# Layer 1's expert loop: the up product in three rounded products instead of one full product, with its halves added by GpSimd

## What is computed

```python
def _peer(h, w_q, sub_keys, expert_u, expert_v):
    ...
        act = jax.nn.gelu(jnp.einsum('td,thkd->thk', tb, expert_u[idx]).astype(jnp.float32),
                          approximate=False)
        w = (gate * act).astype(tb.dtype)
        return jnp.einsum('thk,thkd->td', w, expert_v[idx])
```

## Time and profile before

| what | us |
| --- | --- |
| three runs | 2755.24, 2757.75, 2752.68 (median 2755.24) |
| the profiled execution, own time | 2755.3 |
| its span in the trace | 2753.3 |
| layer 1's expert loop, first to last matmul | 2158.9 to 2732.4 |
| PE busy in the span | 2614.4 (95%) |
| DVE busy | 2260.7 (82%) |
| ACT busy | 1200.7 (44%) |
| POOL busy | 476.4 (17%) |

### The profile page before, as it was taken

The page is one execution under the profiler, slowest core; times in us unless marked ns, Lnnn a source line. Parts: engine busy times, 40 slices in busy tenths (PEclk is TensorE's granted clock), DMA queues, the critical chain, the costliest instruction groups (busy, mean ns, idle before and its releaser), DMA issues.

```text
span 2753.3 us, 48491 instructions
## 1 busy us (share of the span) xinstructions
PE 2614.4 (95%) x16733; PEld 2275.8 (83%) x16733; DVE 2260.7 (82%) x4474; ACT 1200.7 (44%) x2189; POOL 476.4 (17%) x428
## 2 busy tenths in 40 slices
PE   7999999877799999999999998999989999999998
PEld 5878887556788888888888886888979888888887
DVE  6478664999899999999999997797689777777665
ACT  5344442226844444444444445334426533333332
POOL 0000000004533333333333330000004211110010
PEclk8999999888999999999999999999999999999999
DMA  6522322554499999999999993333443699999895
GB/s 268 226 83 98 119 77 107 233 204 143 153 341 371 387 389 386 387 392 382 380 362 370 368 363 139 108 131 104 169 150 134 249 337 340 337 338 329 321 323 200
DMA packets 172367, 708.89 MB, mean 257 GB/s; under 512 B 17088, under 2 KB 50528, under 8 KB 124896
## 3 DMA queue, kind: packets, MB, share of 16 engines
q1 hardware_dynamic: 134480, 431.60, 42.4%
q0 software_dynamic: 37776, 275.83, 27.0%
HBM read 690.61 MB, written 16.65 MB: 257 GB/s over the span
## 4 chain that ended last, share of the span: by engine, by line
PE 81%; DVE 12%; DMA 3%; ACT 2%; issue 2%; SPq 0%; DVEq 0%; ACTq 0%
PE ps L969 81%; DMA ring<-in_w_mod 1%; DVE topi L2675 1%; DVE topi L2683 1%; DVE sc L2677 1%; DMA ring<-in_w_front 1%; DVE top L2680 1%; DVE top L2672 1%; DMA gate_scratch<-spill 1%; DVE elo L2264 0%; DVE rs L2224 0%; DVE loP L2333 0%; DVE gst L2488 0%; PE ps L1121 0%; DVE besti L2683 0%
## 5 line engine op out<-in xcount | busy, mean ns | idle before, releaser
L894 POOL DMA_INDIRECT gbuf<-in_expert_rows,gidx x192 | 277.0, 1443 | 1097.0 <-DVE yg L2846 1080.3
L969 PE MATMUL ps<-h2a,ehi 128*128 128x320 f32 x2048 | 453.0, 309 | 0.0
L2176 ACT ACTIVATE ehi<-ring 128x1024 fp32r<-128x1024 f32 x256 | 271.2, 1059 | 400.0 <-PE ps L969 350.9
L2858 DVE TENSOR_TENSOR elo<-ring,ehi 128x1024 fp32r<-128x1024 f32 x256 | 313.6, 1225 | 136.5 <-ACT ehi L2176 132.2
L969 PE MATMUL ps<-ehi,wA 128*128 128x512 f32 x1280 | 377.2, 392 | 3.5 <-DVE wA L2893 3.5
L969 PE MATMUL ps<-h2b,ring 128*128 128x192 f32 x2048 | 359.7, 326 | 1.0 <-ACT act_ahead L2049 1.0
L969 PEld LDWEIGHTS ps<-h2a,ehi 128*128 128x128 f32 x2048 | 347.7, 188 | 10.3
L969 PEld LDWEIGHTS ps<-h2b,ring 128*128 128x128 f32 x2048 | 338.2, 190 | 10.5 <-issue 1.3
L969 PE MATMUL ps<-h2a,elo 128*128 128x320 f32 x1024 | 316.4, 309 | 0.0
L969 PEld LDWEIGHTS ps<-ehi,wA 128*128 128x128 f32 x1280 | 236.2, 189 | 54.0 <-DVE wA L2893 3.7
L2836 DVE SCALAR_TENSOR_TENSOR gbuf<-gbuf,h2n 128x1024 f32<-128x1024 f32 x192 | 234.4, 1221 | 31.2 <-DMA gbuf<-in_expert_rows,gidx 25.1
(11 more groups left out here) (445 smaller groups left out, 4797.0 us busy)
## 6 DMA issues: line engine op xcount, KB each, us to landing
ring<-in_experts SPq DMA_DIRECT2D x512, 512.0 KB, 6.9
ring<-in_w_mod SPq DMA_DIRECT2D x48, 1024.0 KB, 6.5
ring<-in_w_side SPq DMA_DIRECT2D x24, 1024.0 KB, 5.2
ring<-in_w_front SPq DMA_DIRECT2D x12, 1024.0 KB, 7.5
ring<-in_w_merge SPq DMA_DIRECT2D x16, 768.0 KB, 4.3
ring<-in_w_q SPq DMA_DIRECT2D x12, 1024.0 KB, 7.7
gate_scratch<-spill SPq DMA_DIRECT2D x40, 256.0 KB, 2.0
gateA<-gate_scratch SPq DMA_DIRECT2D x16, 640.0 KB, 8.6
```

The lines of the kernel that those rows point to most:

```text
L894: pool.indirect_dma_start(gbuf[:, k % 2, :], None, a[f"expert_rows{l}"], bass.IndirectOffsetOnAxis(gidx[:, at:at + 1], 0)).then_inc(gather ...
L969: return pe.matmul(out, w, x, start=start, stop=stop, **k)
L2176: act.activation(ehi[:, 2 + k % 2, :], ring[:, (u + k) % RING, DM:2 * DM], ACT.Copy).then_inc(vhi_ready, 1)
L2858: v.tensor_tensor(elo[:, r, DM:2 * DM], ring[:, r, DM:2 * DM], ehi[:, 2 + b, :].bitcast(F32), ALU.subtract).then_inc(vlo_ready, 1)
```

## The change

1. **Up in layer 1** is computed from parts. `h2c` holds the rounded tokens and their remainder side by side. For each of the eight chunks PE does one fp32r matmul of 384 columns (rounded weights against both halves of the tokens) and one of 192 columns (remainder weights against the rounded half). The result stands in 384 columns of PSUM, in two halves that have yet to be added.
2. **ACT** gets `u_high` in layer 1 (the rounded copy of the up weights), and `carry(k + 1)` at the end of step k, which copies the 384 columns from PSUM to `upB`. **POOL** adds the two halves into `actB` and signals `summed`. ACT's Gelu then waits for `summed`.
3. **DVE** gets `u_low` in layer 1. The rounded copy of the gated activations (CAST, 128x192) goes from DVE to ACT, as in layer 0, with the handshake `act_gated` and `whi_ready`. The remainder stays in two operations.
4. **POOL**'s queue holds the additions and gathers in one order: for odd k, gather k // 2 + 2 stands behind the addition of block k.
5. **Constant products** (`keep_on`): bf16 matmuls of 512 columns on the identity, whose result nobody reads, at three kinds of place: 26 behind the mean of layer 1's `norm1`, 12 behind the mean of `norm2` (layer 0's latent pass and layer 1), 8 at the end of layer 0's experts.
6. Before the loop DVE writes `h2c` (two more operations in `norm2`, one copy at the start of `experts`). Buffers move. The semaphores of the two constant loads become one.

```diff
@@ POOL, experts
-                    for k in range(2, gathers(l)):
+                    for k in range(NK if l else 0):
+                        if not is_ahead(l, k):
+                            pool.wait_ge(carried, ups_before(l, k) - NK + 1)
+                            count(pool, w_ready, NK * l + k - 1)
+                            pool.tensor_tensor(actB[:, k % 2, :], upB[:, 0, :], upB[:, 1, :], ALU.add).then_inc(summed, 1)
+                        if k % 2 and k // 2 + 2 < gathers(l):
+                            pool.wait_ge(acc_done, gathers_before(l) + k // 2 + 1)
+                            gather(l, k // 2 + 2)
+                    for k in range(2, 0 if l else gathers(l)):
@@ PE
+            def keep_on(n, bank):
+                one = ident.bitcast(BF16)
+                for _k in range(n):
+                    mm(ps[:, bank, :].rearrange("p (a n) -> p a n", a=2), one[:, 0:P], one.unsqueeze(1).to_broadcast([P, 2, 256]), True, True)
@@ PE, up
+                        pe.wait_ge(ulo_ready, i * per + (ups_before(l, k) + 1))
+                        hi, lo_ = ehi[:, k % 2, :], elo[:, v % RING, 0:DM]
                         if l:
-                            pe.wait_ge(u_in[v % RING], i * 16 + 16 * u_loads(l, k))
                             for c in range(KD):
-                                last = mm(o, ring[:, v % RING, c * P:(c + 1) * P], h2[:, c, :], c == 0, c == KD - 1)
+                                s_ = slice(c * P, (c + 1) * P)
+                                both_ = ps[:, 6 + k % 2, 0:2 * D].rearrange("p (a t) -> p a t", a=2)
+                                mm(both_, hi[:, s_], h2[:, :, c, :], c == 0, False)
+                                last = mm(o, lo_[:, s_], h2[:, 0, c, :], False, c == KD - 1)
@@ ACT, experts
+                    def carry(k, i, per):
+                        act.wait_ge(a_ready, i * per + (ups_before(l, k) + 1))
+                        act.activation(upB[:, :, :], ps[:, 6 + k % 2, 0:384].rearrange("p (a t) -> p a t", a=2), ACT.Copy).then_inc(carried, 1)
@@ ACT, step
+                            if l:
+                                act.wait_ge(summed, i * (RING - is_ahead(l, first)) + (ups_before(l, k) - ub + 2))
+                                act.activation(actT[:, k % 2, :], actT[:, k % 2, :], ACT.Gelu).then_inc(act_ready, 1)
...
-                        if ahead and not l:
-                            u_high(k + 2, i)
-                        if not l:
-                            act.wait_ge(act_gated, i * RING + (k + 1))
-                            act.activation(wh[:, k % 2, :], actT[:, k % 2, :], ACT.Copy).then_inc(whi_ready, 1)
+                        if ahead and not is_ahead(l, k + 2):
+                            u_high(k + 2, i, RING - is_ahead(l, first))
+                        act.wait_ge(act_gated, i * RING + (ub + k + 1))
+                        act.activation(wh[:, k % 2, :], actT[:, k % 2, :], ACT.Copy).then_inc(whi_ready, 1)
...
+                        if l and k + 1 < NK and not is_ahead(l, k + 1):
+                            carry(k + 1, i, RING - is_ahead(l, first))
@@ DVE, norm2
-                        v.tensor_copy(h2[:, :, :], h2T[:, :, 0:w]).then_inc(h2_ready, 1)
+                        v.tensor_copy(h2b[:, :, :], h2T[:, :, 0:w]).then_inc(h2_ready, 1)
+                        link(v.tensor_copy(h2c[:, 1, :, :], h2T[:, :, 0:w]))
+                        v.tensor_tensor(h2c[:, 1, :, :], h2T[:, :, 0:w], h2c[:, 1, :, :].bitcast(F32), ALU.subtract)
@@ DVE, step
-                        if l:
-                            link(v.tensor_tensor(w_, from_, g, ALU.mult))
-                            link(v.tensor_copy(wh[:, b, :], actT[:, b, :]))
-                        else:
-                            v.tensor_tensor(w_, w_, g, ALU.mult).then_inc(act_gated, 1)
-                            if ahead:
-                                u_low(k + 2, i)
-                            dve.wait_ge(whi_ready, i * RING + (k + 1))
+                        v.tensor_tensor(w_, from_ if l else w_, g, ALU.mult).then_inc(act_gated, 1)
+                        if ahead and not is_ahead(l, k + 2):
+                            u_low(k + 2, i, RING - is_ahead(l, first))
+                        dve.wait_ge(whi_ready, i * RING + (ub + k + 1))
@@ DVE, experts
                         dve.wait_ge(ahead_act, AHEAD)
+                        v.tensor_copy(h2c[:, 0, :, :], h2b[:, :, :]).then_inc(h2_ready, 1)
+                        u_low(1, 0)
```

More of the change, by code:

```diff
@@ L436, in build_program @@
         first = ExitStack()
-        h2b = sb("h2b", [P, KD, 192], on=first)
+        lend = ExitStack()
+        h2b = sb("h2b", [P, KD, 192], on=lend)
+        lend.close()
+        h2c = sb("h2c", [P, 2, KD, 192], F32R, on=first)
         idxB = sb("idxB", [P, 3, 192], on=first)
-        actB = sb("actB", [P, 2, 192], on=first)
-        wB = sb("wB", [P, 2, 384], F32R, on=first)
-        whB, wlB = wB[:, :, 0:192], wB[:, :, 192:384]
         act_ahead = sb("act_ahead", [P, IN_ROUTE, 192], on=first)
         first.close()
-        sb("first_space", [P, KD * 2 * DENSE + DM + NK // SLOTS], on=peer)
+        sb("first_space", [P, (2 * KD + 3 + IN_ROUTE) * 192], on=peer)
         h2n = sb("h2n", [P, DM], on=peer)
@@ L455, in build_program @@
         act_more = sb("act_more", [P, AHEAD - IN_ROUTE, 192], on=over)
+        actB = sb("actB", [P, 2, 192], on=over)
         over.close()
@@ L461, in build_program @@
         zeros = sb("zeros", [P, P], on=lend)
+        wB = sb("wB", [P, 2, 384], F32R, on=lend)
+        whB, wlB = wB[:, :, 0:192], wB[:, :, 192:384]
+        upB = sb("upB", [P, 2, 192], on=lend)
         lend.close()
@@ L568, in build_program @@
             sem("lo_ready"), sem("fwh_ready"), sem("fwl_ready"), sem("swh_ready"), sem("swl_ready"))
-        h_rebuilt, x_again = sem("h_rebuilt"), sem("x_again")
+        summed, x_again = sem("summed"), sem("x_again")
         nat_ready, nat_low = sem("nat_ready"), sem("nat_low")
@@ L668, in peer_tiles @@
                 return h2a, idxA, gateA, actA, whA, wlA
-            return h2b, idxB, gateB, actB, whB, wlB
+            return h2c, idxB, gateB, actB, whB, wlB
         def gather_arrived(eng, l, n, i):
@@ L679, in _ @@
         def _(sp):
[L680 to L681 removed]
+            sp.dma_start(par[:, :], a["params"]).then_inc(consts_in, 16)
+            sp.dma_start(cst[:, :], a["consts"]).then_inc(consts_in, 16)
             def load(u, src, i=None, per=0):
@@ L958, in _ @@
                     pool.tensor_tensor(hL, hHi[:, :, CTX:TL].bitcast(F32), hLo1[:, :, CTX:TL].bitcast(F32),
-                                       ALU.add).then_inc(h_rebuilt, 1)
+                                       ALU.add).then_inc(summed, 1)
                 elif kind == "ret" and l == 0:
@@ L1031, in _ @@
                     norm_mean(st, sq1, TL)
+                    keep_on(26, 3)
                 elif kind == "norm2":
@@ L1034, in _ @@
                         norm_mean(st, sq2, 256)
+                        keep_on(12, 4)
                 elif kind == "final":
@@ L1192, in side @@
                         if l:
-                            pe.wait_ge(h_rebuilt, 1)
+                            pe.wait_ge(summed, 1)
                         else:
@@ L1589, in turn @@
                             if not is_ahead(l, k + 1):
-                                up(k + 1, i)
+                                up(k + 1, i, RING - is_ahead(l, first))
                             down(k, i)
@@ L1604, in _ @@
                         if k < RING - 1:
-                            up(k + 1, NK // RING - 1)
+                            up(NK - RING + k + 1, 0)
                         down(k, NK // RING - 1, k == RING - 1)
+                    if not l:
+                        keep_on(8, 6)
                     pe.wait_ge(acc_done, gathers_before(l) + gathers(l))
@@ L1865, in _ @@
                     if l:
-                        act.wait_ge(h_rebuilt, 1)
+                        act.wait_ge(summed, 1)
                     chunks_out(0)
@@ L2136, in _, with u_high @@
                     actT, wh = peer_tiles(l)[3:5]
-                    def u_high(k, i):
-                        act.wait_ge(u_in[(u + k) % RING], i * 16 + 16 * ((ub + k) // RING + 1))
+                    def u_high(k, i, per=RING):
+                        act.wait_ge(u_in[(u + k) % RING], i * 16 + 16 * u_loads(l, k))
                         if k >= 2 or not isinstance(i, int):
-                            act.wait_ge(a_ready, i * RING + (ub + k - 1))
+                            act.wait_ge(a_ready, i * per + ups_before(l, k - 1))
                         act.activation(ehi[:, k % 2, :], ring[:, (u + k) % RING, 0:DM], ACT.Copy).then_inc(uhi_ready, 1)
                     act.wait_ge(x_held, 16 * (l + 1))
+                    u_high(1, 0)
                     if not l:
-                        u_high(1, 0)
                         for parity in range(2):
@@ L2798, in _, with u_low @@
```

(11 more changed lines are left out.)

27 lines of the change are left out of this document (12 added, 15 removed).

## The result

The kernel after takes 2898.12 us (median of 4 runs, 2894.05 to 2900.23) against 2756.49 us for the kernel before on the same chip: ratio 1.0521, 95% interval 1.0503 to 1.0538. The prediction was 2893 (2848 to 2950), slower. The profiled execution of after is its 2894.05 us run.

A forecast was written before the change was run, and what follows sets the result against it. PE bounds the kernel by a small margin over a serial chain through ACT and DVE, which the change lengthens: 2755.3 + 122.8 + 17 + 1.1 - 3.3 = 2892.9 us, range 2848 to 2950.

The forecast's parts named there:

- serial chain, 64 pairs of steps: Layer 1's expert loop: the chain from carry to remainder makes two steps cost 10.88 us, +122.8 us in all.
- clock in the ahead groups: Last step of twenty ahead groups: PE idles 3.7 us, then a half-clock stretch costs some 1.7 us; half taken, +17.
- start of the loop: Start of layer 1's expert loop: `u_high(1)` stands ahead of the table load, +1.1 us on the path.
- norm 2, two places: Constant products in `norm2` fill PE's idle stretch and keep the clock: 1.6 us each, -3.3 us (0 to -4).
- the missing up saves nothing: Ahead groups' last step: the odd chain and the down and up behind stay, so two steps still cost 10.88 us.
- GpSimd's addition is hidden: Layer 1's loop: POOL's addition, about 0.8 us, lies beside v-high's 1.06, with over 1.5 us of cover.
- Rival 2: Up step: 192 columns run at the plain float32 rate, up takes 3.9 us, total 2997 us; chance 0.11.
- Rival 1: Expert loop: PE stays the bound, the chain fitting in one down and one up; 2734.7 us, chance 0.06.
- Rival 3: Even steps: GpSimd's addition gets in ahead of DVE's operations, up to +33 us, so 2926; chance 0.13.
- The copy of `h2c` and `u_low(1)` on DVE lie beside it: Loop start: these two DVE operations run beside `u_high(1)`, whose 1.06 us alone is on the path.

The follow-up runs named there:

- e2: Kernel after plus twelve 512-column bf16 matmuls ahead of the last down step of each ahead group of layer 1: 2854.71 us, ratio 1.0354.
- e5: Kernel after with ScalarE's carry behind the rounding of V and eight 512-column matmuls ahead of each ahead group's last down: 2782.35 us, ratio 1.0101.
- e4: Kernel after with GpSimd's addition of the two up halves replaced by a fill of 0.25: 2897.62 us, ratio 1.0515.
- e1: Kernel after with ScalarE's carry of step k moved behind the rounding of V in the same step: 2803.44 us, ratio 1.0173.
- e3: Kernel before plus twelve 512-column bf16 matmuls behind the mean of norm 2 in both layers: 2747.89 us, ratio 0.9971.
- e8: Kernel before with, in the twelve full groups, a split up step of three 192-column products added in PSUM, plus constant products: 2753.04 us, ratio 0.9979.

## Why the prediction was right, and where it was not

By its own terms, against the profiled executions:

| term | predicted | measured |
|---|---|---|
| serial chain, 64 pairs of steps | +122.8 | 32 x 21.11 - 573.0 = +102.5 |
| clock in the ahead groups | +17 (0 to 34) | 719.8 - 675.5 = +44.3 |
| start of the loop | +1.1 | +2.0 |
| norm 2, two places | -3.3 | -3.1 |
| tail, not foreseen | 0 | -3.2 |
| the rest ahead of the loop, not foreseen | 0 | -3.5 |
| sum | +137.6 | +139.0 |

- **The chain was right in its links and 3% too long.** For the odd step I had 6.16 us; it took 5.88 (in the full groups of after the pairs alternate, 10.99 and 10.11 us, 10.55 in the mean, where I had 10.88). The carry starts 0.19 behind the down, not 0.30, and v-high starts 0.10 before the carry's record ends, an overlap that I had given to DVE's operations and not to ACT's. A down and an up take 4.67 (e2), not 4.72. The claim that the missing up saves nothing is shown by e2.
- **Which link mattered.** e5 against e2 shows that the carry's place ahead of v-high was about 70 of the 101 us by which e2's loop, with the clock up, is longer than before's. That GpSimd's addition is hidden was right (e4); in the odd step v-high lies beside it, as I had said.
- **The clock term was mis-sized**, and this is the step that failed. "a cold stretch of about 3.4 us costs some 1.7 us", and half of twenty places: the idle stretch is 3.41 us, and from the fourth ahead group on every one, 16 in all, had the lower clock for 6.8 us, not 3.4, at 2.8 us each (of the first three, two had it for 3.4 us). The measured 44 lies above the end of 34. I had taken both the length and the frequency from one place, where the engine goes on with other work. In a loop each turn repeats the same idle stretch. That the total still came out within 0.2% is luck: two errors, -20 and +27, that cancel.
- **Rival 2** is out: 384 and 192 columns together take 0.285 to 0.29 us from start to start, and up takes the 2.29 predicted. The two sizes apart were each off and made up for each other: 0.20 and 0.09, where I had 0.175 and 0.112.
- **Rival 1** is wrong for this kernel, but its mechanism exists: e1's full groups have PE busy throughout.
- **Rival 3** is wrong for this kernel and its mechanism is there in e5, where the fill gives back 34 us. That this is near my +33 is chance: I had put it on 44 even steps that are not ahead, and in e5 28 of it lies in the ahead groups, where the addition runs into the odd step's addition of a row. Its sign, longer DVE operations beside the additions, shows in after too (v-low of 1.61 us instead of 1.22) without a price, so the sign alone does not tell.
- **The start of the loop** cost 2.0. "The copy of `h2c` and `u_low(1)` on DVE lie beside it" failed: PE waits for that copy, 2.27 us idle where before has 1.16. The other 0.9 lies between there and the first down (5.47 us against 4.57). Timeline of PE and DVE in after:

```profile
2148.86 1.02 PE L982 MATMUL ps<-zeros 128*128 128x512 bf16 x4 [2.27 <-DVE h2c L2936]
...
2147.65 0.96 DVE L2936 CAST h2c<-h2b 128x1536 fp32r<-128x1536 f32 x1 [2.75 <-ACT act_more L2129]
```

- **Norm 2** was right in the trace. In the medians e3 gained 5 us more than that. The two lengths of the tail can account for up to 3.3. The stretch of layer 1 from its norm 1 to its norm 2 took 304.9 us in before and 301.6 to 303.4 in after and e1 to e4. e3, at 301.6, has before's code there. What the traces show beside it is the clock: it was granted at 0.50 for 13.7 us of that stretch in before, the last time for 3.4 us from 1974.34, for 10.2 us in e3 and not at all in after. That is a part of the 3.3 us; what else is open.

## What to carry to other kernels

Before an instruction that waits for a slow engine is put into an in-order queue, look at what stands behind it: here the copy out of PSUM was cheap (0.49 us), but the rounding behind it waited with it (1.1 us in the step shown), and the whole of VectorE's chain too, and one swap gave back two thirds of the loss, with what it did to the clock. A loop's idle stretch on TensorE has to be priced as one that recurs in every turn, with the clock as the trace shows it after each, and a cost that measures zero in one version (the addition on GpSimd) can be worth over 30 us in the next, so test it again when the cover is gone. And where two versions of a step bound different engines, each kind of group may want its own: the mixture beats both kernels, and e3 by 6 us, by taking the plain up step where there are three of four, and the split one where there are four.

## What was not expected of the hardware

- GpSimd and VectorE hold each other up in both directions. A POOL addition of 0.60 us took 1.65 behind a DVE operation that had started 0.09 us earlier (e5). In e1 it started first and DVE's v-low took 1.61 us, where it takes 1.22 alone (timelines of POOL and DVE):

```profile
2652.88 0.64 POOL L954 TENSOR_TENSOR actB<-upB 128x192 f32<-128x192 f32 x1 [1.59 <-ACT upB L2199]
...
2652.99 1.61 DVE L2894 TENSOR_TENSOR elo<-ring,ehi 128x1024 fp32r<-128x1024 f32 x1
```

  The page "SBUF — State Buffer" of the Trainium skill, section "Who interferes with whom", has the two exclude each other for the whole instruction, whichever starts first, when the DVE operation has two SBUF inputs, as both of these do. The trace agrees in both orders: the later one is longer by about what was left of the earlier (1.19 and 0.53 us left, 1.05 and 0.39 longer).
- The same tail takes 18.1 or 21.4 us from one execution to the next, with the granted clock at 0.84 or 0.74 in the mean. A difference of 3 us between two profiled executions may be this alone.
- A 192-column fp32r product with weights of its own costs 0.11 us from start to start (e8), as much as one of 2 columns; behind a 384-column one it costs 0.088 (after). That the longer product hides its weight load is my reading, not shown.
